# The swap of rotary halves: a permutation matmul replaced by VectorE products and ScalarE copies between groups of 32 partitions

## The chip, the cores and the metric

The kernel runs on all eight cores of one Trainium2 chip. Each core computes 2048 of the 16,384 tokens (batch 2, sequence 8192) and the 128 tokens before them again, so no core waits for another. The time of a run is that of the slowest core in microseconds (us). TensorE (PE) does the matrix products, VectorE (DVE), ScalarE (ACT) and GpSimd (POOL) the elementwise work, and SyncE's queue (SP) starts most transfers.

## The reference, cut to what matters

```python
x = x + 0.5 * swiglu(rmsnorm(x, g1), w_gate1, w_up1, w_down1)
h = rmsnorm(x, g_mix)
glu_a, glu_b, q, k, v, g_conv, g_attn = split(h @ w_in)
conv_out = (silu(layernorm(depthwise_conv31(glu_a * sigmoid(glu_b))))) @ w_proj
q, k = rope(q), rope(k)                # 16 query heads, 4 key/value heads of 64
attn_out = window_attention(q, k, v, sinks) @ w_o        # window of 128
x = x + (sigmoid(g_conv) * conv_out + sigmoid(g_attn) * attn_out) @ w_out
x = x + 0.5 * swiglu(rmsnorm(x, g2), w_gate2, w_up2, w_down2)
out = rmsnorm(x, g_final)

def rope(x):                           # half = 32
    x1, x2 = x[..., :32], x[..., 32:]
    return concat([x1 * cos - x2 * sin, x2 * cos + x1 * sin])
```

## The kernel before, in words

Everything is kept transposed: channels on the 128 partitions, tokens along the free axis. A core works through four tiles (t = 0 to 3) of 512 tokens. A tile passes three parts: FFN 1 (`f_a`, matmuls with inputs xnF and Hh), the mixers (`m_norm`, `m_rest`, inputs xnM, RR, cT, qa, cvo), and FFN 2 (`f_b`, xnF and Hh again). The mixers of tile t run beside FFN 2 of tile t-1 and FFN 1 of tile t+1, so TensorE has FFN matmuls to put between those of the mixers. Weights are streamed through six buffers `wa` and five `wd`: first as float32 over POOL's queue (wall, wd), later from bfloat16 copies over SP's queue (wac, wdc).

The mixers of a tile run in this order: GLU and convolution (lines 852 to 861), keys and values (`kv`, line 688), the sums of the layer norm (`ln_sums`), eight chunks of queries (line 866), sixteen attention units (`attn`, line 779) with one `ln_apply` in every second, gates and projections, and the output projection.

Rotary embedding is done on chunks of 128 channels, two heads, so a half is a group of 32 partitions. Per tile there are ten chunks (two of keys, eight of queries), and tile 0 has two more with 128 tokens. `rope_start` (line 671) projects a chunk into a PSUM bank `pa`, and ScalarE copies it as bfloat16 into a buffer `sq`. `rope_finish` (line 678) multiplies it with the permutation matrix `pswap` on TensorE into a second bank `pr`; VectorE forms t1 = pa * scale * cos and t2 = pr * sin, and GpSimd adds them into `qa` or `kT`. The sign of the sine is in its table (line 1031). For queries, the projection of the next chunk is emitted ahead of the finish of the last one (lines 870 to 873).

The mixers share five PSUM banks, handed out in turn (`bM5`, line 442). In the query loop the order of requests is pa0, pa1, pr0, pa2, pr1, pa3, pr2, and so on. FFN work beside the mixers has three banks (`bF`). The mixers' float32 buffers `tm` are four, also in turn.

The order of work is set before the kernel runs, by a planner (`Plan.schedule`, line 184). Each operation is a task with a planned duration (VectorE 0.7 where none is given, ScalarE 0.62, GpSimd 1.28, a 512-column matmul 0.217), and `join` ties several into one task. The planner keeps a clock for each engine and always places the task that can start first; of equal ones, the one with the lower key (its place in the tile). It adds 0.25 between engines. The result is one fixed list per engine, and on the chip each engine takes its list strictly in order, waiting at semaphores. Those come from `_deps` (line 62), which follows the emitted order and adds one rule that the planner's `_link` (line 154) does not have: an engine that reads a PSUM bank waits for reads of that bank by other engines that were emitted earlier (lines 68 to 71).

Of the kernel before, what the change touches and what calls it, by code (L numbers as in the profile page):

```python
# [7 lines left out]
F32, BF16, I32 = mybir.dt.float32, mybir.dt.bfloat16, mybir.dt.int32  # L8
AF = mybir.ActivationFunctionType
ALU = mybir.AluOpType  # L10
# [326 lines left out]
def build_nc():  # L337
    nc = bass.Bass("TRN2", target_bir_lowering=False)
    dt = nc.dram_tensor
# [6 lines left out]
    w2_d = dt("w2", [8, 128, 1024], F32, kind="ExternalInput").ap()  # L346
    misc_d = dt("misc", [128, 32], F32, kind="ExternalInput").ap()
    ident_d = dt("ident", [128, 128], F32, kind="ExternalInput").ap()
    pswap_d = dt("pswap", [128, 128], F32, kind="ExternalInput").ap()
    outT_d = dt("outT", [D, TOK], F32, kind="ExternalOutput").ap()  # L350
    wac_d = dt("wac", [NBLK_A + 8, 128, 2048], BF16, kind="Internal").ap()
    wdc_d = dt("wdc", [32, 128, 11 * 128], BF16, kind="Internal").ap()
# [2 lines left out]
    with ExitStack() as es:  # L355
        def sb(name, shape, dtype):
            return es.enter_context(nc.sbuf_tensor(name, shape, dtype))
# [8 lines left out]
        POOL = Eng(nc.gpsimd, mksem("s_pool"), 1.28)  # L366
        SP = Eng(nc.sync, mksem("s_sp"))
        G = Plan()
        op, dma = G.op, G.dma
        tt, stt, ts = nc.vector.tensor_tensor, nc.vector.scalar_tensor_tensor, nc.vector.tensor_scalar  # L370
        act, ptt, mm = nc.scalar.activation, nc.gpsimd.tensor_tensor, nc.tensor.matmul
# [27 lines left out]
        wd_hs = [mksem(f"s_wdh{i}") for i in range(ND)]  # L399
        tmF = Banks([(sb(f"tf{i}", [128, NT], F32), Buf()) for i in range(4)])  # L400
        tmM = Banks([(sb(f"tm{i}", [128, NT], F32), Buf()) for i in range(4)])
        sqt = Banks([(sb(f"sq{i}", [128, NT], BF16), Buf()) for i in range(2)])
        sqF = Banks([(sb(f"sx{i}", [128, NT], BF16), Buf()) for i in range(2)])
        accF, accL, accQ = [(sb(f"acc{i}", [128, NT], F32), Buf()) for i in range(3)]
        S = sb("S", [128, 8, 132], F32); S_b = bufs(2)
# [5 lines left out]
        sin_t = sb("sin_t", [128, NT], F32); sin_b = Buf()  # L411
        masks = sb("masks_sb", [128, 4, 128], BF16); masks_b = Buf()
        ident = sb("ident_sb", [128, 128], BF16); ident_b = Buf()
        pswap = sb("pswap_sb", [128, 128], BF16); pswap_b = Buf()
        ones = sb("ones_sb", [128, 128], BF16); ones_b = Buf()
        onesf = sb("onesf_sb", [128, 128], F32); onesf_b = Buf()
        cols = sb("cols_sb", [128, 9, 8], F32); cols_b = Buf()
        hcols = sb("hcols_sb", [128, 9, 8], F32); hcols_b = Buf()
        misc = sb("misc_sb", [128, 32], F32); misc_b = Buf()
# [22 lines left out]
        bM5 = Banks(every[3:8])  # L442
# [4 lines left out]
        def cdma(q, name, dst, src, buf, after=()):  # L447
            dma(q, mksem("s_c_" + name), [(dst, src)], rd=after, wr=(buf,))
# [27 lines left out]
        def ACTF(out, in_, func, rd, wr, t=None, **kw):  # L476
            op(ACT, partial(act, out=out, in_=in_, func=func, **kw), rd, wr, t)

        def STT(out, in0, scalar, in1, op0, op1, rd, wr, t=None):
            op(DVE, partial(stt, out=out, in0=in0, scalar=scalar, in1=in1, op0=op0, op1=op1), rd, wr, t)  # L480
# [7 lines left out]
        def TT(out, in0, in1, o, rd, wr, t=None):  # L488
            op(DVE, partial(tt, out=out, in0=in0, in1=in1, op=o), rd, wr, t)
# [7 lines left out]
        def MM(out, lhsT, rhs, start, stop, rd, wr, t=None):  # L497
            op(PE, partial(mm, out, lhsT=lhsT, rhs=rhs, start=start, stop=stop), rd, wr, t)
# [172 lines left out]
        def rope_start(use, sub, xn_t, xn_bufs, N, scale=1.0):  # L671
            pa, pab = bM5.get()
            proj(pa, pab, use, sub, xn_t, xn_bufs, N)
            qb, qbb = sqt.get()
            ACTF(qb[:, 0:N], pa[:, 0:N], AF.Copy, (pab,), (qbb,), scale=scale)
            return pa, pab, qb, qbb, scale

        def rope_finish(item, c_t, c_b, s_t, s_b, out, obufs, N):
            pa, pab, qb, qbb, scale = item
            pr, prb = bM5.get()  # L680
            MM(pr[:, 0:N], pswap[:], qb[:, 0:N], True, True, (pswap_b, qbb), (prb,))
            t1, t1b = tmM.get()
            t2, t2b = tmM.get()
            STT(t1[:, 0:N], pa[:, 0:N], scale, c_t[:, 0:N], ALU.mult, ALU.mult, (pab, c_b), (t1b,))
            TT(t2[:, 0:N], pr[:, 0:N], s_t[:, 0:N], ALU.mult, (prb, s_b), (t2b,))
            PTT(out, t1[:, 0:N], t2[:, 0:N], ALU.add, (t1b, t2b), obufs)

        def kv(t):
# [242 lines left out]
        load_pos(HALO, NT, cos_t, cos_b, (H_b[4],))  # L931
        load_x(1, (H_b[8],))
        cdma(POOL, "ident", ident[:], ident_d, ident_b, (H_b[11],))
        cdma(POOL, "pswap", pswap[:], pswap_d, pswap_b)
        cdma(POOL, "masks", masks[:], masks_d, masks_b)
        G.key = -0.6
        rope_tables(HALO, cos_h, cosh_b, sin_h, sinh_b)
# [19 lines left out]
def _pack_shared(inp):  # L957
    f = np.float32
    w_in = np.asarray(inp["w_in"][0], f)
    bnds = np.cumsum([1024, 1024, 1024, 256, 256, 1024, 1024])  # L960
    glu_a, glu_b = w_in[:, :bnds[0]], w_in[:, bnds[0]:bnds[1]]
    wq, wk, wv = w_in[:, bnds[1]:bnds[2]], w_in[:, bnds[2]:bnds[3]], w_in[:, bnds[3]:bnds[4]]
    g_conv, g_attn = w_in[:, bnds[4]:bnds[5]], w_in[:, bnds[5]:bnds[6]]

    def rot(wh):
        n = wh.shape[1] // 64
        return wh.reshape(D, n, 2, 32)[:, :, ::-1, :].reshape(D, n * 64)

    def qchunk(w, qc):
        gp, i = qc // 4, qc % 4  # L970
        h0, h1 = 4 * (2 * gp) + i, 4 * (2 * gp + 1) + i
        return np.concatenate([w[:, h0 * 64:(h0 + 1) * 64], w[:, h1 * 64:(h1 + 1) * 64]], axis=1)

    blocks = []

    def ffn_blocks(wg, wu):
        for b in range(NFC):
            blocks.append(np.concatenate([wg[:, 128 * b:128 * b + 128], wu[:, 128 * b:128 * b + 128]], axis=1))

    ffn_blocks(np.asarray(inp["ffn1_w_gate"][0], f), np.asarray(inp["ffn1_w_up"][0], f))  # L980
    blocks.append(wk)
    blocks.append(wv)
    for j in range(4):
        blocks.append(np.concatenate([qchunk(wq, 2 * j), qchunk(wq, 2 * j + 1)], axis=1))
    for cc in range(8):
        blocks.append(np.concatenate([glu_a[:, 128 * cc:128 * cc + 128], glu_b[:, 128 * cc:128 * cc + 128]], axis=1))
    w_cp = np.asarray(inp["conv_w_proj"][0], f)
    w_o = np.asarray(inp["attn_w_o"][0], f)
    perm = np.zeros(D, np.int64)
    for hc in range(8):  # L990
        gp, i = hc // 4, hc % 4
        for e in range(2):
            h = 4 * (2 * gp + e) + i
            perm[hc * 128 + e * 64:hc * 128 + e * 64 + 64] = np.arange(h * 64, h * 64 + 64)
    w_o_p = w_o[perm, :]
    for dc in range(8):
        blocks.append(np.concatenate([g_conv[:, 128 * dc:128 * dc + 128], g_attn[:, 128 * dc:128 * dc + 128]], axis=1))
        blocks.append(np.concatenate([w_cp[:, 128 * dc:128 * dc + 128], w_o_p[:, 128 * dc:128 * dc + 128]], axis=1))
    w_out = np.asarray(inp["w_out"][0], f)
    for j in range(4):  # L1000
        blocks.append(w_out[:, 256 * j:256 * j + 256])
    ffn_blocks(np.asarray(inp["ffn2_w_gate"][0], f), np.asarray(inp["ffn2_w_up"][0], f))
    assert len(blocks) == NBLK_A
    wall = np.stack([np.asarray(b, f).reshape(8, 128, 256).transpose(1, 0, 2).reshape(128, 2048) for b in blocks], axis=0)
    wall = np.ascontiguousarray(wall)
    wd = np.stack([np.asarray(inp["ffn1_w_down"][0], f), np.asarray(inp["ffn2_w_down"][0], f)], axis=0)
    wd = wd.reshape(2, 2, 11, 128, 8, 128).transpose(0, 4, 1, 3, 2, 5)
    wd = np.ascontiguousarray(wd.reshape(32, 128, 11 * 128))

    gate_b = np.asarray(inp["gate_b"][0], f)  # L1010
    vecs = [inp["ffn1_norm"][0], inp["mix_norm"][0], inp["ffn2_norm"][0], inp["final_norm"], inp["conv_dw_b"][0],
            inp["conv_ln_g"][0], inp["conv_ln_b"][0], gate_b[:1024], gate_b[1024:]]
    cols = np.stack([np.asarray(v, f).reshape(8, 128) for v in vecs], axis=0)
    cols = np.ascontiguousarray(cols.transpose(2, 0, 1))
    dw = np.zeros((32, D), f)
    dw[32 - CW:] = np.asarray(inp["conv_dw_w"][0], f)
    dw = dw.reshape(8, 4, 8, 4, 32)
    w2 = np.zeros((8, 4, 32, 4, 8, 32), f)
    ii = np.arange(32)
    w2[:, :, ii, :, :, ii] = dw.transpose(4, 2, 1, 3, 0)  # L1020
    w2 = np.ascontiguousarray(w2.reshape(8, 128, 1024))
    misc = np.zeros((128, 32), f)
    p = np.arange(128)
    inv_freq = (np.float32(10000.0) ** (-np.arange(32, dtype=f) / np.float32(32))).astype(f)
    misc[:, 0] = inv_freq[p % 32]
    misc[:, 1] = np.where((p % 64) < 32, -1.0, 1.0)
    sinks = np.asarray(inp["attn_sinks"][0], f)
    misc[:, 2] = EPS
    misc[:, 3] = LN_EPS
    misc[:, 4] = np.pi / 2  # L1030
    for gp in range(2):
        for i in range(4):
            for e in range(2):
                misc[:, 16 + gp * 8 + (i // 2) * 4 + e * 2 + i % 2] = sinks[4 * (2 * gp + e) + i]
    ident = np.eye(128, dtype=f)
    pswap = np.zeros((128, 128), f)
    mm = np.arange(128)
    pswap[np.where((mm % 64) < 32, mm + 32, mm - 32), mm] = 1.0
    return dict(wall=wall, wd=wd, cols=cols, w2=w2, misc=misc, ident=ident, pswap=pswap)

def _masks(first):
    q = np.arange(128)[:, None]
# [35 lines left out]
```

How the kernel before makes its waits and increments, by code:

```python
    def wait(self, sem, val):  # L40
        if val <= 0:
            return
        if sem is self.sem:
            if val > sem.n or not SAME_ENGINE_SYNC or self.no_self:
                return
        if self.known.get(sem, 0) >= val:
            return
        self.e.wait_ge(sem.h, val)
        self.known[sem] = val
# [29 lines left out]
def emit_op(eng, fn, rd=(), wr=()):  # L79
    for s, v in _deps(rd, wr, eng.sem).items():
        eng.wait(s, v)
    inst = fn()
    eng.sem.n += 1
    inst.then_inc(eng.sem.h, 1)
    ev = eng.sem.n
    for b in wr:
        b.w = {eng.sem: ev}
        b.r = {}
    for b in rd:
        if b.r.get(eng.sem, 0) < ev:
            b.r[eng.sem] = ev
# [1 line left out]
def emit_dma(q, dsem, moves, rd=(), wr=()):  # L93
    for s, v in _deps(rd, wr, None).items():
        q.wait(s, v)
    q.wait(dsem, dsem.n)
    for out_ap, in_ap in moves:
        q.e.dma_start(out=out_ap, in_=in_ap).then_inc(dsem.h, 16)
        dsem.n += 16
    for b in wr:
        b.w = {dsem: dsem.n}
        b.r = {}
    for b in rd:
        b.r[dsem] = dsem.n
```

## Time and profile before

| | us |
|---|---|
| median of 3 runs | 1834.73 (1834.13 to 1840.92) |
| the profiled execution | 1835.85 |
| its span, slowest core (core 7) | 1834.8 |
| spans of the eight cores | 1814.7 to 1834.8 |
| PE busy | 1668.5 (91%) |
| DVE, ACT, POOL busy | 709.8, 651.3, 690.0 (39%, 35%, 38%) |

The span is the time from a core's first to its last instruction; about 1 us of the execution lies outside it. PE's busy time is modelled for overlapping matmuls: a lone 512-column matmul is shown with 379 ns, but in a dense row they start some 216 ns apart. The same holds in a smaller way for DVE and ACT, whose next instruction can start before the last has ended. So durations and distances between starts are both read. All rows below are of core 7.

### The profile page before, as it was taken

The numbers are of one execution on the slowest core, as the hardware profiler recorded it, in microseconds if no ns is written. First come the engines' busy times: TensorE is split into PE (matmuls) and PEld (weight loads), VectorE is DVE, ScalarE is ACT, GpSimd is POOL, SyncE is SP. The second block draws the span as 40 slices with busy tenths as digits, with TensorE's granted clock in tenths as the row PEclk, the third lists the DMA queues.
The fourth block names the chain that finished last, engine by engine and source line by source line (L and its number), as shares of the span: only waits on it lengthen the run. The fifth ranks groups of instructions, "written<-read, shape, count | busy, mean of one in ns | idle before, by whom it ended". The sixth has DMA issues, their size and how long they took to land.

```text
span 1834.8 us, 29585 instructions; the slowest of 8 cores (1814.7 to 1834.8 us)
## 1 busy us (share of the span) xinstructions
PE 1668.5 (91%) x9060; PEld 747.1 (41%) x9060; DVE 709.8 (39%) x1180; ACT 651.3 (35%) x1396; POOL 690.0 (38%) x727
## 2 busy tenths in 40 slices
PE   6989878898987889789999999999998999998997
PEld 3545334343433334334443344444443444443442
DVE  3431523753152266332225267532214356524212
ACT  3211413653221266333322247543222257513221
POOL 1113136754331396423331377422322277322221
PEclk9989888899998999899999999999999999998987
DMA  9987899669898897976754987673443953444432
GB/s 180 195 183 139 177 202 196 166 163 222 165 201 194 197 188 153 178 200 199 198 146 145 230 225 176 156 236 133 158 140 113 247 164 121 148 141 142 155 102 100
DMA packets 121001, 315.39 MB, mean 172 GB/s; under 512 B 14864, under 2 KB 36624, under 8 KB 120848
## 3 DMA queue, kind: packets, MB, share of 16 engines
q1 hardware_dynamic: 94784, 231.47, 40.0%
q0 software_dynamic: 25344, 80.95, 27.6%
q8 instruction: 78, 1.28, 0.3%
q10 hardware_dynamic: 720, 1.09, 0.2%
q14 instruction: 75, 0.61, 0.1%
HBM read 327.01 MB, written 67.37 MB: 215 GB/s over the span
## 4 chain that ended last, share of the span: by engine, by line
PE 76%; DMA 14%; issue 3%; DVE 2%; ACT 2%; POOL 2%; SPq 1%; DVEq 0%; ACTq 0%; POOLq 0%
PE ps L501 70%; PE ps L82 4%; DMA wa<-wall 4%; DMA X<-xT 2%; DMA wa<-wac 1%; DMA outT<-tf 1%; DMA wd<-wd 1%; SPq L98 1%; DMA wdc<-wd 1%; DMA RR<-ush 1%; DMA ush<-uT 1%; DMA ush<-S 1%; PE ps L699 1%; DMA wac<-wa 1%; DMA wd<-wdc 1%
## 5 line engine op out<-in xcount | busy, mean ns | idle before, releaser
L501 PE MATMUL ps<-xnF,wa 128*128 128x512 bf16 x2816 | 669.0, 393 | 40.4 <-DMA wa<-wall 17.2
L501 PEld LDWEIGHTS ps<-xnF,wa 128*128 128x128 bf16 x2816 | 274.2, 100 | 395.6 <-issue 119.1
L501 PE MATMUL ps<-Hh,wd 128*128 128x512 bf16 x1408 | 341.3, 391 | 17.0 <-DMA wd<-wd 10.0
L501 PE MATMUL ps<-xnM,wa 128*128 128x512 bf16 x1344 | 313.8, 385 | 6.2 <-DMA wa<-wac 3.8
L82 ACT ACTIVATE tf<-ps 128x512 f32<-128x512 f32 x304 | 180.0, 595 | 346.4 <-PE ps L501 320.0
L82 POOL TENSOR_TENSOR Hh<-tf 128x512 bf16<-128x512 f32 x128 | 165.1, 1292 | 200.6 <-PE ps L501 126.7
L82 DVE SCALAR_TENSOR_TENSOR tf<-tf,ps 128x512 f32<-128x512 f32 x176 | 120.2, 684 | 307.8 <-PE ps L501 269.2
L501 PEld LDWEIGHTS ps<-Hh,wd 128*128 128x128 bf16 x1408 | 136.9, 100 | 187.3 <-issue 59.1
L501 PEld LDWEIGHTS ps<-xnM,wa 128*128 128x128 bf16 x1344 | 130.9, 99 | 177.1 <-issue 31.4
L82 DVE SCALAR_TENSOR_TENSOR X<-ps,X 128x512 f32<-128x512 f32 x96 | 66.3, 691 | 224.4 <-PE ps L501 215.6
L98 POOL DMA_DIRECT2D wa<-wall x117 | 65.2, 559 | 217.5 <-PE ps L501 177.1
L82 ACT ACTIVATE S<-S,sm 128x129 f32<-128x129 f32 x256 | 103.1, 403 | 65.4 <-DVE sm L82 46.8
L82 POOL TENSOR_TENSOR acc<-acc,tf 128x512 f32<-128x512 f32 x56 | 70.9, 1265 | 109.7 <-ACT tf L82 106.6
L82 DVE SCALAR_TENSOR_TENSOR tm<-tm,ps 128x512 f32<-128x512 f32 (+1 forms) x86 | 50.1, 584 | 156.9 <-PE ps L501 150.6
L82 POOL TENSOR_TENSOR P<-S,sm 128x512 bf16<-128x512 f32 x64 | 67.0, 1046 | 80.0 <-DVE sm L82 41.7
L82 POOL TENSOR_TENSOR acc<-acc,tm 128x512 f32<-128x512 f32 x56 | 70.7, 1263 | 67.7 <-ACT tm L82 67.5
L82 POOL TENSOR_TENSOR cvo<-tm 128x512 bf16<-128x512 f32 x32 | 40.5, 1267 | 136.9 <-DVE tm L82 136.7
L82 POOL TENSOR_TENSOR cvo<-cvo,acc 128x512 f32<-128x512 f32 x64 | 83.2, 1305 | 10.2 <-ACT acc L82 9.0
L501 PE MATMUL ps<-RR,wa 128*32 128x512 bf16 x1024 | 65.5, 403 | 23.1 <-DMA RR<-ush 19.0
L82 ACT ACTIVATE tm<-ps,hcols_sb 128x512 f32<-128x512 f32 x64 | 43.4, 686 | 111.5 <-PE ps L501 102.1
L82 ACT ACTIVATE tf<-X 128x512 f32<-128x512 f32 x56 | 35.1, 626 | 132.7 <-DVE X L82 106.6
L82 ACT ACTIVATE tm<-cvo 128x512 f32<-128x512 f32 (+1 forms) x67 | 39.5, 593 | 117.6 <-DVE cvo L82 114.2
(100 smaller groups left out, 1548.7 us busy)
## 6 DMA issues: line engine op xcount, KB each, us to landing
wa<-wac SPq DMA_DIRECT2D x195, 512.0 KB, 4.7
wa<-wall POOLq DMA_DIRECT2D x117, 512.0 KB, 9.0
wac<-wa SPq DMA_DIRECT2D x78, 512.0 KB, 8.0
wd<-wdc SPq DMA_DIRECT2D x80, 352.0 KB, 4.1
RR<-ush SPq DMA_DIRECT2D x128, 135.0 KB, 5.2
wd<-wd POOLq DMA_DIRECT2D x48, 352.0 KB, 7.5
wdc<-wd SPq DMA_DIRECT2D x32, 352.0 KB, 5.5
X<-xT SPq DMA_DIRECT2D x28, 256.0 KB, 9.7
```

Of the source, the lines that this page charges most:

```text
L82: inst = fn()
L98: q.e.dma_start(out=out_ap, in_=in_ap).then_inc(dsem.h, 16)
L501: op(PE, lambda: mm(out, lhsT=pick(use.slot), rhs=rhs, start=start, stop=stop), rd, wr, t, use)
L699: op(PE, lambda kc=kc: mm(pst[:, 0:256], lhsT=xn_t[:, kc, c0:c0 + 128], rhs=uv.slot[:, kc, 0:256], start=(kc == 0), stop=(kc == 7)), (xn_b ...
```

## The change: what it does

The matrix `pswap`, its transfer and its bfloat16 copy go, and with them the copies into `sq` and the 42 permutation matmuls. In their place, in `rope_finish`:

- for the lower 64 partitions, two VectorE instructions on 32 partitions each read `pa` at the partition group that is the other half of the pair, multiply by scale and sine, and write t2;
- for the upper 64 partitions, two ScalarE copies on 32 partitions each bring the other half (float32, scaled) from `pa` into the bank `pr`, and one VectorE product over 64 partitions forms the rest of t2;
- t1 is as before, and is joined with the first two products into one task of the planner. The two copies are another joined task, planned at 0.6 each.

The copies are now in `rope_finish`, so they are emitted after the next chunk's projection; `rope_start` holds the projection alone. The banks are asked for in the same order as before.

```diff
-        pswap = sb("pswap_sb", [128, 128], BF16); pswap_b = Buf()
-        sqt = Banks([(sb(f"sq{i}", [128, NT], BF16), Buf()) for i in range(2)])
...
         def rope_start(use, sub, xn_t, xn_bufs, N, scale=1.0):
             pa, pab = bM5.get()
             proj(pa, pab, use, sub, xn_t, xn_bufs, N)
-            qb, qbb = sqt.get()
-            ACTF(qb[:, 0:N], pa[:, 0:N], AF.Copy, (pab,), (qbb,), scale=scale)
-            return pa, pab, qb, qbb, scale
+            return pa, pab, scale
 
         def rope_finish(item, c_t, c_b, s_t, s_b, out, obufs, N):
-            pa, pab, qb, qbb, scale = item
-            pr, prb = bM5.get()
-            MM(pr[:, 0:N], pswap[:], qb[:, 0:N], True, True, (pswap_b, qbb), (prb,))
+            pa, pab, scale = item
             t1, t1b = tmM.get()
             t2, t2b = tmM.get()
+            pr, prb = bM5.get()
+            G.join(True)
+            for d in (64, 96):
+                ACTF(pr[d:d + 32, 0:N], pa[d ^ 32:(d ^ 32) + 32, 0:N], AF.Copy, (pab,), (prb,), t=0.2 + 0.4 * N / 512, scale=scale)
+            G.join(False)
+            G.join(True)
+            for d in (0, 32):
+                STT(t2[d:d + 32, 0:N], pa[d ^ 32:(d ^ 32) + 32, 0:N], scale, s_t[d:d + 32, 0:N], ALU.mult, ALU.mult, (pab, s_b), (t2b,))
             STT(t1[:, 0:N], pa[:, 0:N], scale, c_t[:, 0:N], ALU.mult, ALU.mult, (pab, c_b), (t1b,))
-            TT(t2[:, 0:N], pr[:, 0:N], s_t[:, 0:N], ALU.mult, (prb, s_b), (t2b,))
+            G.join(False)
+            TT(t2[64:128, 0:N], pr[64:128, 0:N], s_t[64:128, 0:N], ALU.mult, (prb, s_b), (t2b,))
             PTT(out, t1[:, 0:N], t2[:, 0:N], ALU.add, (t1b, t2b), obufs)
...
-        cdma(POOL, "pswap", pswap[:], pswap_d, pswap_b)
```

## Rows read from the trace of the kernel before

**Rows 1.** The page: TensorE's and DMA's lines of the 40 slices.
```profile
PE   6989878898987889789999999999998999998997
PEclk9989888899998999899999999999999999998987
DMA  9987899669898897976754987673443953444432
```

**Rows 2.** The page: the chain that ended last, by engine.
```profile
PE 76%; DMA 14%; issue 3%; DVE 2%; ACT 2%; POOL 2%; SPq 1%; DVEq 0%; ACTq 0%; POOLq 0%
```

**Rows 3.** Groups by form: operation, out<-in, count | busy us, mean ns | idle before, releasers.
```profile
L82 PE MATMUL ps<-sq,pswap_sb 128*128 128x512 bf16 x40 | 15.2, 379 | 0.6 <-ACT sq L82 0.6
L82 PE MATMUL ps<-sq,pswap_sb 128*128 128x128 bf16 x2 | 0.4, 216 | 0.1
L82 ACT ACTIVATE sq<-ps 128x512 bf16<-128x512 f32 x40 | 23.7, 594 | 31.8 <-PE ps L501 31.1 <-DVE tm L82 0.8
L82 ACT ACTIVATE sq<-ps 128x128 bf16<-128x128 f32 x2 | 0.6, 278 | 1.3 <-PE ps L699 1.3
L82 DVE SCALAR_TENSOR_TENSOR tm<-ps,cos_t 128x512 f32<-128x512 f32 x40 | 27.6, 690 | 30.1 <-PE ps L501 16.8 <-POOL qa L82 9.9 <-PE ps L699 3.1
L82 DVE SCALAR_TENSOR_TENSOR tm<-ps,S 128x128 f32<-128x128 f32 x2 | 0.6, 291 | 1.7 <-PE ps L82 1.0 <-PE ps L699 0.7
L82 ACT ACTIVATE tm<-ps,hcols_sb 128x512 f32<-128x512 f32 x64 | 43.4, 686 | 111.5 <-PE ps L501 102.1 <-POOL cvo L82 4.8 <-DVE tm L82 3.6
```

**Rows 4.** Timeline of TensorE, queries of tile 3: start, us, operation.
```profile
1494.17 0.38 PE L82 MATMUL ps<-sq,pswap_sb 128*128 128x512 bf16 x1
1494.38 1.89 PE L501 MATMUL ps<-xnM,wa 128*128 128x512 bf16 x8
1496.11 0.38 PE L82 MATMUL ps<-sq,pswap_sb 128*128 128x512 bf16 x1
...
1549.48 5.35 PE L501 MATMUL ps<-xnF,wa 128*128 128x512 bf16 x24
```

**Rows 5.** Timeline of VectorE, tile 2, queries and start of attention.
```profile
1086.35 0.69 DVE L82 SCALAR_TENSOR_TENSOR tm<-ps,cos_t 128x512 f32<-128x512 f32 x1 [0.99 <-POOL qa L82]
1086.96 0.68 DVE L82 TENSOR_TENSOR tm<-ps,sin_t 128x512 f32<-128x512 f32 x1
1087.58 0.69 DVE L82 SCALAR_TENSOR_TENSOR tm<-ps,cos_t 128x512 f32<-128x512 f32 x1
1088.55 0.69 DVE L82 TENSOR_TENSOR tm<-ps,sin_t 128x512 f32<-128x512 f32 x1 [0.28 <-PE ps L82]
...
1090.77 6.46 DVE L82 SCALAR_TENSOR_TENSOR cT<-tm,cvo 128x512 bf16<-128x512 f32 x1 [0.93 <-ACT tm L82]
1097.15 0.72 DVE L82 COPY_PREDICATED S<-masks_sb,ps 128x512 f32<-128x512 uint16 x1
1097.97 0.69 DVE L82 TENSOR_REDUCE sm<-S 128x4 f32<-128x516 f32 x1
...
1101.11 0.18 DVE L82 RECIPROCAL sm<-sm 128x4 f32<-128x4 f32 x1 [0.66 <-ACT S L82]
```

**Rows 6.** Timeline of ScalarE, the same stretch.
```profile
1098.75 0.41 ACT L82 ACTIVATE S<-S,sm 128x129 f32<-128x129 f32 x1 [5.28 <-DVE sm L82]
...
1100.82 0.19 ACT L82 ACTIVATION_READ_ACCUMULATOR S<-S,sm 128x1 f32 x1
...
1101.39 1.07 ACT L82 ACTIVATE tf<-ps 128x512 f32<-128x512 f32 x2
```

**Rows 7.** Windows: PE, PEld, DVE, ACT, POOL busy, clock, DMA, GB/s; queries of tiles 1, 2, 3.
```profile
647.00:662.40 15.40, 14.72 (x69) 6.47 (x67) 9.23 (x15) 7.11 (x12) 15.17 (x15) 1.00 0.97 193
1075.00:1085.00 10.00, 10.00 (x48) 4.50 (x47) 7.44 (x12) 4.17 (x7) 9.79 (x10) 1.00 0.80 168
1490.00:1504.20 14.20, 14.20 (x69) 6.27 (x66) 9.30 (x14) 6.21 (x12) 12.91 (x12) 1.00 0.39 128
```

**Rows 8.** Timeline of TensorE, start of attention, tiles 0, 1, 2, then tile 3.
```profile
327.97 0.61 PE L82 MATMUL ps<-kT,qa 64*128 64x256 bf16 x4 [3.30 <-DVE S L82]
328.52 8.09 PE L501 MATMUL ps<-xnF,wa 128*128 128x512 bf16 x24
...
354.45 0.75 PE L82 MATMUL ps<-PT,V 128*64 128x256 bf16 x4 [3.34 <-DVE PT L82]
...
673.30 0.38 PE L82 MATMUL ps<-ident_sb,P 128*128 128x128 bf16 x4 [2.66 <-POOL P L82]
...
1098.01 0.41 PE L82 MATMUL ps<-kT,qa 64*128 64x256 bf16 x4 [4.02 <-DVE S L82]
1098.36 7.04 PE L501 MATMUL ps<-xnF,wa 128*128 128x512 bf16 x24
...
1534.53 1.89 PE L501 MATMUL ps<-xnF,wa 128*128 128x512 bf16 x8 [0.51 <-ACT tf L82]
```

More of the change, by code:

```diff
@@ L348, in build_nc @@
     ident_d = dt("ident", [128, 128], F32, kind="ExternalInput").ap()
-    pswap_d = dt("pswap", [128, 128], F32, kind="ExternalInput").ap()
     outT_d = dt("outT", [D, TOK], F32, kind="ExternalOutput").ap()
@@ L1035, in _pack_shared @@
     ident = np.eye(128, dtype=f)
[L1036 to L1039, printed above, removed]
+    return dict(wall=wall, wd=wd, cols=cols, w2=w2, misc=misc, ident=ident)
 def _masks(first):
```

## The prediction

> **What bounds the kernel now.** I read the page's slices first. TensorE is busy nine tenths or more in nearly all of the second half, while DMA falls to three to five tenths there; in the first half DMA is at seven to nine tenths and TensorE has gaps [rows 1]. The chain of waits puts 76% on PE and 14% on DMA [rows 2]. So the second half, tiles 2 and 3, is bound by TensorE, and the first partly by weight transfers. A matmul taken away is worth its full place on PE only where PE is dense.
>
> Then the groups by form, for what the change touches [rows 3], the timelines of the query stage for the distances between starts [rows 4 to 6], and the windows for the room beside it [rows 7]. In the query stages PE is full (14.72 of 15.40, 10.00 of 10.00, 14.20 of 14.20), DVE is at 60, 74 and 65% and POOL at 99, 98 and 91%. Last, what PE waits for where attention begins [rows 8].
>
> **What it removes.** 42 matmuls, 40 of them of 512 columns. The profile gives one 379 ns, but that is a modelled end: from one permutation matmul to the next, nine matmuls apart, are 1496.11 - 1494.17 = 1.94 us, so one costs 0.216 [rows 4]. 40 x 0.216 = 8.6 us, and two of 128 columns, at a quarter to the full distance, 0.1 to 0.4. Together 8.8 us off PE. Their weight loads lie under other matmuls. PE waited only 0.6 us for their inputs in all [rows 3], so no stall goes with them. Where PE is at half clock the saving doubles, but the query stages of tiles 1 to 3 are at 1.00 [rows 7]. The transfer of the matrix is one of hundreds and I give it nothing; at most it frees one short slot on POOL's queue.
>
> **What it adds.** None of the new operations is in the trace: all work on 32 or 64 partitions, and three move data between partition groups. For a VectorE product of 512 columns the nearest rows are t1 and t2, at 0.69 us each and 0.61 from start to start [rows 3, 5]. If time followed the amount of data, the 128x128 form at 0.29 would be the nearest below; if a shifted read were as bad as the worst product here, it would be the 6.46 of cT [rows 5]. I take 0.61 between starts and 0.69 for the last, since that row has the same columns, types and memories. For a ScalarE copy of 512 columns the rows are 0.594 alone, two in 1.07 (0.48 between starts), 0.686 with a bias and 0.278 for 128 columns [rows 3, 6]; I take two in 1.07.
>
> Per chunk of 512 columns VectorE goes from two instructions (1.22) to four (2.44), which is 40 x 1.22 = 49 us more on an engine with 1,125 us idle. ScalarE goes from one copy to two, 40 x 0.48 = 19 us more. GpSimd has the same adds. None of this is on PE by itself. But in the query stage a chunk cost PE 1.94, and costs it 1.73 now (nine places less one), against 2.44 on VectorE: there VectorE becomes the slower one, and eight chunks take it 19.5 us instead of the some 14 seen for the whole stage. The planner knows this, for it counts 4 x 0.7 = 2.8 a chunk, and will put FFN matmuls into the difference, 8 x (2.8 - 1.73) = 8.6 us, two or three FFN blocks of 3.46. Those are not lost: in tile 3 a lot of FFN work is left when the attention begins, and the attention units are spread over it by their keys. If that cover were gone it would be 8.6 us a tile, 34 in all.
>
> The Trainium skill, VectorE: DVE Perf Modes, section "Two Vector instructions with no wait between them", speaks against the change: an instruction whose input or output starts in another group of 32 partitions than the one before it starts only when all earlier ones have ended. Every one of the four instructions of a chunk does so, and the next instruction after them. The trace before has no such case: its starts are 0.61 apart at a duration of 0.69 [rows 5]. By the rule the four take 4 x 0.69 = 2.8 and the loop below 0.16 more a chunk, 5 us over the kernel before cover.
>
> **What it moves.** The planner does not know that readers of one PSUM bank on two engines take turns; the semaphores enforce it. Both engines now read `pa`, the copies on ScalarE first as they can start first, and VectorE's three after them. Also the bank for `pr` of chunk n is the one that held `pa` of chunk n-1 (five banks in turn), so ScalarE can't begin before VectorE has finished its three instructions of chunk n-1. That makes a loop through two engines. From the end of VectorE's three for one chunk: 0.1 to ScalarE (1098.66 to 1098.75), 1.07 for the two copies, 0.1 back (1101.01 to 1101.11), then 0.61 + 0.61 + 0.69 = 1.91, in all 3.2 us [rows 5, 6]. The one product of 64 partitions fits under the copies. The plan has 2.8 for it. So a chunk ends 0.4 later than planned each time, and the first one 1.2 later: 1.2 + 7 x 0.4 = 4.0 us a tile, 16 us for four tiles. Before, ScalarE's one copy was out of the way long before VectorE came (VectorE idled 0.3 to 1.0 us a chunk [rows 5]), so this did not show.
>
> Queued behind the waiting VectorE and ScalarE instructions are the FFN's tanh, copy and product, which free the three FFN banks, and the next attention unit. PE takes its list in order, so it stands when one of those banks or the first queries are late. Between nothing (the FFN's VectorE instructions that lie inside the loop fill the wait, and PE has 1.07 a chunk of other work) and the full 4.0 us a tile, I take half, 2.0 a tile, as the loop has about one FFN instruction of VectorE every second chunk. That is 8 us. The keys' two chunks a tile have value projections behind them on PE and I give them nothing; without that cover it is 1.2 each.
>
> **The sum.** -8.8 + 8 = -0.8 us on the profiled 1835.85, which itself is 1.1 above the median; on the median 1834.73 this is 1834.
>
> **Rivals.**
>
> *The saving stands.* For it: VectorE has room in all windows, and FFN instructions fill the loop. Then PE has 8.8 us less to do: 1826. More is possible. The stalls where attention begins come from a single product, cT from two SBUF operands, that takes 6.46 instead of 0.68 while GpSimd runs without a pause [rows 5]; they stop PE for 3.30, 3.34, 2.66 and 4.02 us, and after two of them 24 matmuls take 8.09 or 7.04 instead of 5.35 [rows 4, 8]. In the change, GpSimd's adds come 2.8 apart instead of 1.94 and its queue is emptier by then. If two of those stalls go, with 1.7 to 2.7 of slow clock each, it is 10 us more: 1816. Against it: such stalls depend on how the lists happen to meet, and can as well grow.
>
> *The loop reaches PE whole; the kernel is slower.* Place: VectorE and ScalarE taking turns on `pa` in the eight query chunks of each tile. Price: 4 x 4.0 = 16 us, with the late first queries making one stall of 3 us or more at the start of attention, after which matmuls ran slowly for 1.7 to 2.7 us [rows 4, 8], 4 x 2.2 = 9. 16 + 9 - 8.8 = +16: 1851. With VectorE's starts 0.69 apart it is 4 x 1.1 = 5 more, 1856. It decides from 2.2 us of stall a tile on, where it has eaten the saving; from 4.5 a tile it is measurable. For it: the order is fixed, and PE is dense, so what is late by more than the plan's margin shows at once. Against it: the plan's 0.25 between engines is 0.1 on the chip, and its 0.7 is 0.61.
>
> *It is hidden anyway.* In tiles 0 and 1 the PE waits for weights after the mixers, so time saved or lost there returns in a transfer wait. Only tiles 2 and 3 count, 20 matmuls, -4.3 us, or with half the loop -0.3: 1830 to 1834, inside my own case.
>
> **Chances and range.** Within 0.5% (9.2 us, about what a measurement of this kernel can tell from no change) lie my forecast and the hidden case, 1825.6 to 1843.9: 0.38. The saving with fewer stalls, faster by over 0.5%, 0.29: the plain saving falls just inside the bound, and needs some luck with the stalls. Slower by over 0.5%, 0.33. The range goes from 1816 (saving and two stalls gone) to 1858 (the loop whole, held starts); the likeliest case's own is 1826 to 1844.
>
> **What would show it.** The forecast is right if PE has 42 matmuls less, DVE's busy time grows by about 40 x 1.38 = 55 us and ACT's by some 20 to 24, VectorE's copies of the pattern three-then-one show 3.2 a chunk or more with waits on ScalarE between, and PE has new stalls of 1 to 3 us a tile in and just after the query stage. If the three products follow each other without a wait for ScalarE, the loop is wrong and the first rival holds. If PE stands 4 us or more a tile on queries or FFN banks, and the granted clock falls behind it, the second holds. It would all be wrong if a product on 32 partitions with a shifted read took far from 0.69, or if the new lists shift weight transfers so that DMA waits of PE change by more than 10 us.

## The result, and the profile after

The changed kernel is slower: the ratio to the kernel before is 1.0204 (95% interval 1.0167 to 1.0241), some 38 us. Three executions took 1869.8 to 1875.5 us, the profiled one 1873.54 (span 1872.5, core 5). In the other three one die ran at a granted clock of 0.79 to 0.84, which the kernel before showed too in some of its runs, and every time and ratio in this document leaves such runs out.

The changed kernel's page, to be laid beside [rows 1, 2]: the 40 slices and the chain that ended last.

```profile
PE   6989767897987879889999887998999998999897
PEclk9999889999998989999999999999998999999898
DMA  9988988769898868875654966675443853353533
...
PE 69%; DMA 15%; DVE 6%; issue 4%; ACT 3%; SPq 2%; POOL 1%; DVEq 0%; ACTq 0%; POOLq 0%
```

PE has lost a tenth or two where the queries and the start of attention of a tile lie (slices 7, 15, 23 to 25 and 34; five other slices lost a tenth and three gained one), and the chain has 6% on DVE in place of 2%, 7% less on PE. The groups by form that the change made (operation, out<-in, shapes, count | busy us, mean ns | idle before and what ended it):

```profile
L82 DVE SCALAR_TENSOR_TENSOR tm<-ps,sin_t 32x512 f32<-32x512 f32 x80 | 54.5, 681 | 38.2 <-ACT ps L82 21.0 <-PE ps L498 8.2 <-POOL acc L82 2.7
L82 DVE TENSOR_TENSOR tm<-ps,sin_t 64x512 f32<-64x512 f32 x40 | 27.8, 694 | 5.7 <-ACT ps L82 4.6
L82 DVE SCALAR_TENSOR_TENSOR tm<-ps,cos_t 128x512 f32<-128x512 f32 x40 | 27.7, 691 | 1.3
L82 ACT ACTIVATE ps<-ps 32x512 f32<-32x512 f32 x80 | 45.4, 568 | 47.2 <-DVE tm L82 30.6 <-PE ps L498 9.8 <-PE ps L701 2.8
```

A product on 32 partitions takes 681 ns, as long as one on 128 (690 in [rows 3]); what a VectorE or ScalarE instruction costs here goes by its 512 columns, not by its partitions. New is the idle time: 21.0 us of VectorE's ended by ScalarE, 30.6 us of ScalarE's ended by VectorE. That is the loop. In tile 3 it looks like this on VectorE (start, us, operation, idle before):

```profile
1541.57 1.47 DVE L82 SCALAR_TENSOR_TENSOR tm<-ps,sin_t 32x512 f32<-32x512 f32 x2 [0.77 <-ACT ps L82]
1543.07 0.69 DVE L82 SCALAR_TENSOR_TENSOR tm<-ps,cos_t 128x512 f32<-128x512 f32 x1
1543.79 0.69 DVE L82 TENSOR_TENSOR tm<-ps,sin_t 64x512 f32<-64x512 f32 x1
1545.25 1.47 DVE L82 SCALAR_TENSOR_TENSOR tm<-ps,sin_t 32x512 f32<-32x512 f32 x2 [0.77 <-ACT ps L82]
```

and on ScalarE:

```profile
1540.17 1.23 ACT L82 ACTIVATE ps<-ps 32x512 f32<-32x512 f32 x2 [2.52 <-DVE tm L82]
...
1543.86 1.23 ACT L82 ACTIVATE ps<-ps 32x512 f32<-32x512 f32 x2 [1.73 <-DVE tm L82]
```

A chunk takes 1545.25 - 1541.57 = 3.68 us, where the forecast had 3.2. Two terms were short: the copies take 1.23 a pair and not 1.07, and the three products 2.19 (1541.57 to 1543.76) and not 1.91, as their starts are 0.71 to 0.79 apart. On TensorE, the same stretch:

```profile
1531.74 7.07 PE L498 MATMUL ps<-xnM,wa 128*128 128x512 bf16 x32
1541.16 3.12 PE L498 MATMUL ps<-xnM,wa 128*128 128x512 bf16 x8 [2.35 <-DVE tm L82]
1544.08 2.38 PE L498 MATMUL ps<-xnF,wa 128*128 128x512 bf16 x8
1546.30 1.89 PE L498 MATMUL ps<-xnM,wa 128*128 128x512 bf16 x8
1548.03 5.34 PE L498 MATMUL ps<-xnF,wa 128*128 128x512 bf16 x24
1557.90 0.54 PE L82 MATMUL ps<-kT,qa 64*128 64x256 bf16 x4 [4.53 <-DVE tm L82]
1559.35 3.25 PE L498 MATMUL ps<-xnF,wa 128*128 128x512 bf16 x8 [0.91 <-DVE tf L82]
```

PE projects four chunks at once, then stands until a bank is free; it has 32 FFN matmuls to do after that, and stands 4.53 us in front of the first scores. The 8 matmuls at 1541.16 and at 1559.35 take 3.12 and 3.25 instead of 1.89: after each of the two stalls the granted clock was at the lower of its two levels, 1.2 GHz, for a while (its mean is 0.59 from 1541.1 to 1544.1 and 0.57 from 1559.3 to 1562.6). The four stages from the last value projection to the first scores, in windows (PE, PEld, DVE, ACT, POOL busy, clock, DMA share, GB/s), with the sum of the same stages before in the last line:

```profile
298.60:338.10 39.50, 31.78 (x150) 14.58 (x150) 27.71 (x46) 22.48 (x39) 27.38 (x28) 1.00 0.75 148
647.70:681.10 33.40, 29.87 (x124) 12.73 (x124) 22.50 (x34) 19.70 (x31) 24.52 (x23) 0.90 0.67 142
1096.00:1131.50 35.50, 26.50 (x122) 11.68 (x122) 25.24 (x38) 20.70 (x32) 25.84 (x23) 0.96 0.56 131
1523.10:1557.90 34.80, 27.91 (x122) 12.33 (x123) 23.96 (x36) 19.70 (x31) 23.49 (x19) 0.95 0.34 106
sum 143.20, PE 116.05 PEld 51.32 DVE 99.42 ACT 82.59 POOL 101.24; mean PE 29.01 PEld 12.83 DVE 24.85 ACT 20.65 POOL 25.31
...
sum 102.50, PE 101.85 PEld 48.24 DVE 53.58 ACT 53.57 POOL 77.18; mean PE 25.46 PEld 12.06 DVE 13.39 ACT 13.39 POOL 19.29
```

Before, the same four stages took 102.5 us with PE busy for 101.85. Now they take 143.2 with 27 us of it idle. Over the whole kernel, the gaps in PE's timeline by what ended them, mean of the eight cores: VectorE 23.2 us before and 53.9 after (+30.7), ScalarE 33.4 and 34.6, GpSimd 19.4 and 21.2, transfers 78.7 and 81.8; in all 155.9 and 192.7. So PE has 37 us more idle time and 8.8 us less work, and the mean span grew by 34.8. Of the 7 us between, 3 are clock: PE's busy time at a lowered clock, times what the clock lacked to 1, is 58.5 us before and 61.8 after. The rest was not traced.

### The profile page after: what moved, and what is told of

Read it like the earlier page. It is cut to its first block, busy times and chain, and to the rows that moved or that the text cites. A ratio compares the mean times of both kernels' runs of the same rounds, so it can differ in the third digit from the quotient of the medians.

```text
span 1872.5 us, 29671 instructions; the slowest of 8 cores (1840.5 to 1872.5 us)
## 1 busy us (share of the span) xinstructions
PE 1655.4 (88%) x9018; PEld 740.6 (40%) x9018; DVE 764.9 (41%) x1264; ACT 674.4 (36%) x1438; POOL 690.2 (37%) x726
## 3 DMA queue, kind: packets, MB, share of 16 engines
q8 instruction: 77, 1.26, 0.3%
## 4 chain that ended last, share of the span: by engine, by line
PE 69%; DMA 15%; DVE 6%; issue 4%; ACT 3%; SPq 2%; POOL 1%; DVEq 0%; ACTq 0%; POOLq 0%
PE ps L498 65%; PE ps L82 4%; DVE tm L82 4%; DMA wa<-wall 3%; DMA wa<-wac 2%; DMA X<-xT 2%; DMA ush<-uT 2%; ACT ps L82 2%; SPq L98 2%; DMA RR<-ush 1%; DMA wdc<-wd 1%; DMA wd<-wd 1%; DMA ush<-S 1%; DVE S L82 1%; DMA wd<-wdc 1%
## 5 line engine op out<-in xcount | busy, mean ns | idle before, releaser
L498 PE MATMUL ps<-Hh,wd 128*128 128x512 bf16 x1408 | 331.1, 383 | 17.9 <-DMA wd<-wdc 9.7
L98 POOL DMA_DIRECT2D wa<-wall x117 | 65.5, 561 | 227.4 <-PE ps L498 192.7
```

What stands on the lines that cost most here:

```text
L98: q.e.dma_start(out=out_ap, in_=in_ap).then_inc(dsem.h, 16)
L498: op(PE, lambda: mm(out, lhsT=pick(use.slot), rhs=rhs, start=start, stop=stop), rd, wr, t, use)
```

## The experiments

Two questions: does the loop cost the time, and through what. All ratios are to the kernel before on the same chip; 1% is 18.4 us.

**The two sides of the change, one at a time.** `b_noswap` is the kernel before without copies and matmuls:

```diff
-            ACTF(qb[:, 0:N], pa[:, 0:N], AF.Copy, (pab,), (qbb,), scale=scale)
-            MM(pr[:, 0:N], pswap[:], qb[:, 0:N], True, True, (pswap_b, qbb), (prb,))
-            TT(t2[:, 0:N], pr[:, 0:N], s_t[:, 0:N], ALU.mult, (prb, s_b), (t2b,))
+            TT(t2[:, 0:N], pa[:, 0:N], s_t[:, 0:N], ALU.mult, (pab, s_b), (t2b,))
```

> The kernel before with the 42 permutation matmuls and the 42 ScalarE copies in front of them left out; VectorE multiplies pa itself by the sine, so the halves are not exchanged. Everything else, and the order in which banks are asked for, is as before. Theory 1 (the added loop between ScalarE and VectorE costs the time, the removed matmuls bring what was forecast): 8.8 us less than before, within 3 us, as PE is dense in the query stages. Rival 2 (the lists of the planner re-roll by far more than 8.8 us whenever a task changes, and the 38 us are such a re-roll): anything from 20 faster to 20 slower than before.

Measured: 0.9871 (0.9845 to 0.9897), 24 us faster, nearly three times what was expected. `b_nomm` keeps the copies and leaves out the matmuls alone:

> The kernel before without the 42 permutation matmuls but with the ScalarE copies (whose result nobody reads); VectorE multiplies pa itself by the sine, so the halves are not exchanged. Leaving out both gave 24 us. Theory A (TensorE's place is the saving, PE being the bound): 18 to 26 us faster than before, the copies being free. Theory B (the copies and their turns on pa cost the other 15): 7 to 12 us faster.

Measured: 0.9957 (0.9933 to 0.9981), 8 us. The forecast's first term, 8.8 us for the 42 matmuls, stands. The copies on ScalarE are worth another 16 us in the kernel before (9 to 22 by the two intervals). PE's idle time ended by VectorE is 23.9 us with them and 15.8 without, which is half of it; where the other half goes was not found.

`b_dve2` adds VectorE's share of the change to the kernel before and leaves the swap on TensorE:

```diff
+            G.join(True)
+            for d in (0, 32):
+                STT(t2[d:d + 32, 0:N], pa[d ^ 32:(d ^ 32) + 32, 0:N], scale, s_t[d:d + 32, 0:N], ALU.mult, ALU.mult, (pab, s_b), (t2b,))
             STT(t1[:, 0:N], pa[:, 0:N], scale, c_t[:, 0:N], ALU.mult, ALU.mult, (pab, c_b), (t1b,))
+            G.join(False)
```

> The kernel before, whole, with the two shifted VectorE products on 32 partitions added ahead of t1 and joined with it (the later full product overwrites their result). VectorE has then more work a chunk (four instructions, 64 us more in all) than in the changed kernel, but ScalarE has one copy a chunk, emitted early, and the second bank is filled by TensorE. Theory 1 (it is the loop: copies on ScalarE wait for VectorE of the chunk before, VectorE waits for the copies): at most a third of the loss, so 0 to 13 us slower than before. Rival 3 (it is VectorE's load in the query stage, with or without ScalarE): 30 us or more slower. The starts of the shifted products are 0.72 to 0.75 us apart if the hold between partition groups is what stretched them.

Measured: 1.0066 (1.0043 to 1.0089), 12 us slower. The shifted products start 0.79 apart and t1 0.71 after the second, so the mean is as expected. VectorE's busy time, 758.9 us, is nearly that of the changed kernel (764.9), so a third of the loss comes with the load and two thirds come with something else.

**Undoing the loop by banks.** `a_banks` asks for `pr` next to `pa`:

```diff
             pa, pab = bM5.get()
+            bank = bM5.get()
             proj(pa, pab, use, sub, xn_t, xn_bufs, N)
```

> The changed kernel with the bank pr asked for right after pa, before the projection. With five banks in turn, pr of chunk n is then the bank that held pa of chunk n-2 and not n-1, so ScalarE's copies need not wait for VectorE's three instructions of the chunk before. All instructions are the same. Theory 1: a chunk takes VectorE's own 2.9 us in place of 3.68, its waits for ScalarE of 0.77 a chunk are gone, and half to all of the 38 us come back: 1840 to 1855. Rival 3 (VectorE's load): no gain over 5 us, 1868 to 1876.

Measured: 1.0183 (1.0149 to 1.0217). A miss: in the second half of the stage a chunk did take 2.95 us (1544.88 to 1547.83 in tile 3, without a wait), but nothing came back. PE's idle time ended by VectorE is 47.5 us in place of 53.9, but that ended by ScalarE is 41.8 in place of 34.6 and by transfers 87.3 in place of 81.8. So the loop's length is not the price by itself.

**Telling the planner.** `a_link` gives the planner the rule of the semaphores:

```diff
         for b in rd:
             k.after.update(b.pw)
+            if b.psum:
+                k.after.update(a for a in b.pr if a.eng is not k.eng)
```

> The changed kernel, with the planner told of the rule that the semaphores follow: a task that reads a PSUM bank comes after the reads of other engines that were made before it. No instruction and no semaphore rule changes, only the order of the lists. Theory 1 (PE stands because the planner put too little FFN work beside a loop that it did not see): the loop stays at 3.7 us a chunk, PE's stalls at the queries and the start of attention shrink, and half to all of the loss comes back: 1838 to 1855. Rival 3 (the loop's length itself is the cost, whatever lies beside it): 1865 to 1880.

Measured: 1.0037 (1.0014 to 1.006). Four fifths of the loss is gone, with every instruction still there. PE's timeline in the query stage of tile 3:

```profile
1509.77 7.07 PE L500 MATMUL ps<-xnM,wa 128*128 128x512 bf16 x31
1516.68 1.89 PE L500 MATMUL ps<-xnF,wa 128*128 128x512 bf16 x8
1518.41 1.89 PE L500 MATMUL ps<-xnM,wa 128*128 128x512 bf16 x8
1520.13 3.62 PE L500 MATMUL ps<-xnF,wa 128*128 128x512 bf16 x16
1523.59 1.89 PE L500 MATMUL ps<-xnM,wa 128*128 128x512 bf16 x8
1525.53 10.31 PE L500 MATMUL ps<-xnF,wa 128*128 128x512 bf16 x47
1535.77 0.39 PE L82 MATMUL ps<-kT,qa 64*128 64x256 bf16 x4
```

and its four stages together:

```profile
sum 141.40, PE 136.97 PEld 63.13 DVE 104.92 ACT 95.95 POOL 120.57; mean PE 34.24 PEld 15.78 DVE 26.23 ACT 23.99 POOL 30.14
```

The stages are as long as in the changed kernel (141.4 and 143.2), but PE is busy for 137 us of them in place of 116, so 4 us of them are idle in place of 27. Between the last value projection and the first scores the lists have 104, 72, 88 and 88 FFN matmuls of 512 columns in tiles 0 to 3, against 64, 48, 48 and 48 in the changed kernel and 32, 24, 32 and 24 before. (`b_dve2` has 64, 48, 48 and 48 as well, but its stages are 18 us shorter in all, and only 5 us of them are idle.) 144 more, at 0.216 us, are 31 us, which is also the gain (31 us). That the two agree so well is chance: in the two versions with a later key below the same sum gives 17 us for a gain of 27, and 36 for 30.

Two controls ask whether any new plan moves the time so far. `b_link` has the same two lines in the kernel before; `b_roll` has GpSimd planned at 1.26 in place of 1.28.

> Control: the kernel before, with only the planner told that readers of one PSUM bank on two engines take turns. Theory 1 (blindness of the planner matters where the copy and the product meet late, as in the changed kernel): before had slack there, so within 8 us of before. Rival 4 (the rule helps any version equally, and the gain of some 27 us with it in the changed kernel is no sign of the loop): 15 us or more faster than before.

> Control for the re-roll: the kernel before with the planner's duration of GpSimd operations at 1.26 in place of 1.28, nothing else; the measured mean is 1.27. All lists are planned anew. Rival 2 (any new plan moves the time by tens of us): 15 us or more either way. Theory 1: within 6 us of before.

Measured: 0.9988 (0.9967 to 1.0008) and 0.9986 (0.9952 to 1.0019), neither clear of 1. For the kernel before, a new plan by itself moved the time by less than 9 us either way. For the changed kernel no such control was run, and the next group shows that small changes of its planned durations move more.

**Right durations.** `a_linkcost` and `a_cost` plan the copies at 0.62 and the three products at 0.75 each, with and without the rule; `b_dve2cost` does that for `b_dve2`.

```diff
-...AF.Copy, (pab,), (prb,), t=0.2 + 0.4 * N / 512, scale=scale)
+...AF.Copy, (pab,), (prb,), t=0.62 * N / 512, scale=scale)
-...ALU.mult, ALU.mult, (pab, s_b), (t2b,))
+...ALU.mult, ALU.mult, (pab, s_b), (t2b,), t=0.75)
```

> The changed kernel with the planner told of the readers' turns and of the durations that the trace shows: 0.62 a copy on 32 partitions, 0.75 for each of the three products (start to start 0.72 to 0.75 when the partition group changes). Theory 1: the plan then meets the chip, PE's idle time that VectorE ends goes from 31 us (with the rule alone) towards the 22 us of before, and the time to 1830 to 1845, not slower than with the rule alone. Rival 3 (what is left is the length of the loop, not the plan): no gain over the rule alone, 1840 to 1850.

> The changed kernel with the measured durations in the plan (0.62 a copy, 0.75 a shifted product and t1) and without the rule on readers. The plan has then 2.95 a chunk on VectorE, the chip 3.68. Theory 1 with the turns as the larger part: the loss of 38 us shrinks by a third at most, 1857 to 1872. Rival 5 (it was the durations, and the rule only lengthened the plan in the same way): as fast as with both, 1837 to 1848.

> The kernel before with the two shifted products added, planned now at 0.75 for each of the three joined instructions. Without this it was 12 us slower than before. Theory 1: the 12 us are the 0.15 a chunk by which the plan fell short, and it comes to within 5 us of before. Rival 3: still 9 to 15 us slower, as the load stays.

Measured: 1.0023 (0.9998 to 1.0048) with the rule, 1.0306 (1.0274 to 1.0338, from two runs) without, and for `b_dve2cost` two runs of 1864.55 and 1868.02 us, which give no interval, against 1853.0 to 1856.5 for `b_dve2` on another chip (the kernel before has a median of some 1838 us on the chip of `b_dve2cost` and some 1841 on that of `b_dve2`). With the rule, PE's idle time that VectorE ends did not fall as expected: it is 32 us, as with the rule alone (33). The other two are plain misses, and they refuted the theory in its first form, that PE stands because the plan is shorter than the chip: better durations made it worse. `a_dve` and `a_dvecost` say the same. All four shifted products are on VectorE, no engine takes turns on `pa`, and the second is planned at 3.75 a chunk, where the chip takes 3.81:

```diff
-            for d in (64, 96):
-                ACTF(pr[d:d + 32, 0:N], pa[d ^ 32:(d ^ 32) + 32, 0:N], AF.Copy, ...)
-            for d in (0, 32):
+            for d in (0, 32, 64, 96):
                 STT(t2[d:d + 32, 0:N], pa[d ^ 32:(d ^ 32) + 32, 0:N], ...)
-            TT(t2[64:128, 0:N], pr[64:128, 0:N], s_t[64:128, 0:N], ALU.mult, (prb, s_b), (t2b,))
```

> The changed kernel with all four shifted products on VectorE (five instructions a chunk, 3.7 us) and no ScalarE copies; the bank is still asked for and left unused. No engine takes turns with another on pa. Planned at 3.5, so the plan misses only 0.2 a chunk, 8 us in all, against 0.9 a chunk in the changed kernel. Theory 1 (turns that the plan does not know): faster than the changed kernel by 10 us or more, 1845 to 1862, though VectorE has 29 us more to do. Rival 3 (VectorE's load in the query stage): slower than the changed kernel, 1875 to 1890.

> The version with all shifted products on VectorE, planned at 0.75 for each of the five instructions (3.75 a chunk, the chip takes 3.7) in place of 0.7. No turns between engines, so this tells whether a plan short by 0.2 a chunk costs what was seen (34 us slower than before). Theory 1 (PE's stalls come from the plan falling behind the chip, whatever the reason): most of the loss goes, 1835 to 1850. Rival 3 (VectorE's load as such): 1865 to 1880.

Measured: 1.0185 (1.0154 to 1.0215) and 1.0209 (1.018 to 1.0238). With no loop at all the loss is the same. That doesn't make the loop free: a chunk still takes 3.81 us here, by VectorE's five instructions alone, where the loop had 3.68. What these versions share with the changed kernel stands in PE's timeline, here `a_dve` in tile 3:

```profile
1519.69 5.34 PE L498 MATMUL ps<-xnF,wa 128*128 128x512 bf16 x24
1524.87 12.25 PE L498 MATMUL ps<-xnM,wa 128*128 128x512 bf16 x56
1536.96 8.80 PE L498 MATMUL ps<-xnF,wa 128*128 128x512 bf16 x40
1553.68 0.61 PE L82 MATMUL ps<-kT,qa 64*128 64x256 bf16 x4 [7.92 <-DVE tm L82]
```

64 FFN matmuls, then nothing to do. In the lists it is 64, 32, 64, 64 with either duration, and for `b_dve2cost` 64, 48, 24, 32, less than the 64, 48, 48, 48 of `b_dve2`. That gave the second theory: the planner books VectorE for the rotary tasks, which have the lower key, without a hole; the FFN's product, which frees the three FFN banks, comes after them; so there are no FFN matmuls to lay beside. The rule would help because with it the plan shows VectorE waiting for ScalarE, and the FFN's products go into those holes. The traces agree with the theory here: VectorE does 5, 3, 4 and 4 of the FFN's products (tf<-tf,ps) in the four stages of `a_link`, but 2, 1, 2 and 1 in the changed kernel, no more than in the kernel before, whose stages are 9 to 12 us shorter.

The theory does not cover everything. `a_cost` has 64, 48, 56 and 56 FFN matmuls in its lists, more than the changed kernel, and 25 us of idle time in the stages, about the same, and yet it is 19 us slower. Its PE waits 9 us more on ScalarE and 5 more on VectorE, and the longer waits lie in the attention that follows. Why was not found.

**Only the order of the FFN's work.** `a_key`, `a_dvekey` and the control `b_key` change one number, the key of VectorE's rotary task:

```diff
+            keep, G.key = G.key, G.key + 0.3
             G.join(True)
             for d in (0, 32):
...
+            G.key = keep
             PTT(out, t1[:, 0:N], t2[:, 0:N], ALU.add, (t1b, t2b), obufs)
```

> The changed kernel, without the rule on readers and with the old durations; only VectorE's joined task of the rotary products has its key later by 0.3 of a tile, so that of tasks ready together VectorE takes the FFN's first. From the last value projection to the first score matmul the plan then has 72, 64, 80, 72 FFN matmuls of 512 columns in tiles 0 to 3, against 64, 48, 48, 48 in the changed kernel and 104, 72, 88, 88 with the rule. Theory 2 (the loss is that too few FFN matmuls stand beside the longer stage, because the FFN's VectorE work comes last there): about two thirds of the way to the version with the rule, 1845 to 1858. Theory 1 (the plan must know the turns): no gain over 8 us, 1864 to 1876.

> The version with all shifted products on VectorE, old durations, with the same later key on its joined task. FFN matmuls in the stage: 128, 80, 80, 104 against 64, 32, 64, 64. Theory 2: from 34 us slower than before to 10 to 22 slower, 1844 to 1858. Rival 3 (VectorE's load as such): still 28 or more slower, 1865 and up.

> Control: the kernel before with the later key on t1's task. The stage is full there, its FFN matmuls are 32, 24, 40, 24 against 32, 24, 32, 24. Theory 2: within 6 us of before. If it is 12 or more faster, the key is good by itself and says nothing on the change.

Measured: 1.0055 (1.0034 to 1.0075), 1.0024 (1.0006 to 1.0042), which is better than the 10 to 22 us of loss expected, and 1.0015 (0.9988 to 1.0041). The loop is untouched in `a_key`: VectorE's waits for ScalarE in it are 27.7 us against 27.3 in the changed kernel:

```profile
DVE tm L82 <- ACT ps L82: 27.7, 28, 2.4
```

and yet 27 of the 38 us are back. With all products on VectorE it is 30 of 34. No instruction differs between `a_key` and the changed kernel, or between `a_dvekey` and `a_dve`, so what the added operations cost hangs on the order of the lists, and putting the FFN's VectorE work ahead takes most of the cost away. The FFN's products in the four stages are 4, 3, 4 and 4 in `a_key`.

How the time comes back is only in part what the theory says. The four stages of `a_key` together:

```profile
sum 155.90, PE 134.82 PEld 58.69 DVE 112.94 ACT 88.76 POOL 112.60; mean PE 33.71 PEld 14.67 DVE 28.23 ACT 22.19 POOL 28.15
```

They hold more work, but they are also longer, and 21 us of them are still idle, 6 fewer than in the changed kernel. Over the whole kernel, mean of the eight cores, PE's idle time is 13 us less than in the changed kernel (179.3 for 192.7), and the mean granted clock is 0.961 in place of 0.952: what PE's busy time lost to a lowered clock is 49.1 us in place of 61.8, another 13. Together they make the 25 us by which the mean span is shorter. In `a_link` it is 17 us of idle time (175.5) and 8 of clock (53.6). So less idle time in the query stage is shown with the rule; with the key, half of the gain is clock, most of it in the attention after the stage. `a_key`'s PE still stands 42 us on VectorE over the kernel, against 33 with the rule. That this rest is the plan's ignorance of the turns is likely but not shown, as the two times differ by only 3 us.

**Better versions?** `a_early` has rule, durations, and the copies emitted with the projection:

> The changed kernel with rule and measured durations, and with the ScalarE copies emitted with the projection, as the copy of the kernel before is, and the bank pr asked for next to pa. The copies no longer wait for VectorE of the chunk before, and VectorE no longer for them; a chunk can take VectorE's own 2.95. FFN matmuls in the stage: 64, 88, 72, 72, enough for 8 chunks at 2.95. Theory 2: stage short and filled, 1832 to 1843, as fast as before or up to 6 us faster, since 8.8 us of TensorE work are gone. If the length of the stage doesn't matter once it is filled: the same as with rule and durations, 1838 to 1848.

Measured: 1.013 (1.0088 to 1.0171). A miss: PE stands 47 us on VectorE. Tile 3's stage is short and full as expected (29.5 us, no idle time), but tile 0's list has only 64 FFN matmuls in 40 us, and after the stage more stalls follow. Its lists have 296 FFN matmuls in the four stages, more than the 288 of `a_key`, which is faster, and it has the rule. So neither the count nor the rule is enough by itself. Why this plan comes out so was not pursued. The last two add the key to the versions with rule and durations, and to `a_dvecost`:

> The changed kernel with the rule on readers, the measured durations and the later key together; FFN matmuls in the stage 112, 96, 104, 96 against 104, 80, 80, 96 without the key. Theory 2: PE's idle time that VectorE ends goes from 31 us to 23 to 28, and the time to 0 to 0.2% of before, 1835 to 1844; if it were filled to the full, the 8.8 us of TensorE work would show as 1830.

> All shifted products on VectorE, with the key and 0.75 for each of the five instructions; FFN matmuls in the stage 144, 88, 88, 104 against 128, 80, 80, 104 without the durations. Theory 2: 0 to 0.3% above before, 1835 to 1846. If VectorE's load as such were the rest, 10 us or more above, as it has 67 us more work than before.

Measured: 1.0011 (0.9984 to 1.0037) and 1.0014 (0.9992 to 1.0037). Both are even with the kernel before and no better. In `a_linkkey` PE's idle time that VectorE ends stayed at 32 us, where 23 to 28 were expected.

Taken together, the changed kernel and its four versions with neither rule nor key (`a_banks`, `a_cost`, `a_dve`, `a_dvecost`) lie 1.8 to 3.1% above the kernel before, the six with rule, key or both 0.1 to 0.6%, and `a_early`, with the rule, 1.3%.

## Why the prediction was wrong

*The saving.* Right: 8.8 us forecast for the 42 matmuls, 8 measured with them alone left out. That the copies beside them cost nothing was wrong; with them gone too it was 24.

*The added operations.* Durations right to 5%: 681 and 694 ns for 690, 568 for 594. VectorE's busy time grew by 55.1 us (forecast 55), ScalarE's by 23.1 (forecast 20 to 24). Distances were short. The shifted products start 0.71 to 0.79 apart, where the forecast took 0.61. By the Trainium skill, VectorE: DVE Perf Modes, section "Two Vector instructions with no wait between them", an instruction that starts in another group of 32 partitions than the one before it is held until all earlier ones have finished; the forecast named this only as an alternative. The trace agrees with that rule: each start comes 0.03 to 0.10 us after the end of the instruction before, at least 0.71 apart, wherever the partition group changes, and 0.61 apart where it does not, here from t1 to another product on 128 partitions in tile 2:

```profile
1101.31 0.69 DVE L82 SCALAR_TENSOR_TENSOR tm<-ps,cos_t 128x512 f32<-128x512 f32 x1
1101.92 0.68 DVE L82 SCALAR_TENSOR_TENSOR acc<-ps,acc 128x512 f32<-128x512 f32 x1
```

In the loop the two copies on ScalarE don't overlap either: 1.23 for the pair, where two copies on 128 partitions took 1.07 [rows 6].

*The loop.* Right in place, order and cause: banks and readers in turn, 3.68 us a chunk for 3.2. That its lateness against the plan is what costs the time was wrong: without the loop (`a_dve`) the loss is the same, and with the loop whole (`a_key`) most of it is gone.

*The cover.* This is the step that failed. "The planner knows this, for it counts 4 x 0.7 = 2.8 a chunk, and will put FFN matmuls into the difference, 8 x (2.8 - 1.73) = 8.6 us, two or three FFN blocks of 3.46. Those are not lost". It put in 16 to 32 matmuls more a tile, 3.5 to 7 us, and there it stopped. The stage grew by 9 to 12 us a tile, so 27 us stayed empty in the four, where 1 us had been. The FFN's matmuls need their banks freed by VectorE, the slower engine of that stage now, and VectorE did no more FFN products in the longer stages than before (2, 1, 2 and 1). The price for a lost cover was in the text (8.6 a tile, 34 in all); I took it for hidden and booked 8 us of stall where VectorE ended 31 more. With that in place of the 8 the sum gives -8.8 + 31 = +22; PE's other waits grew by 6 and the clock took 3, which makes 31 of the 35 by which the mean span grew.

*The second rival* had the right sign and half of the size (1851 to 1856 for 1873), partly by luck: it had 16 us of stall for 31 and 9 us of slow clock for 3, and its cause, the loop reaching PE, is not the one that the runs show.

*The first rival* laid all four stalls at the start of attention to the product cT. One of them was read wrongly: the 2.66 in tile 1 was ended by GpSimd's P, and the two cT products there took 2.81 together.

*The hold on FFN banks.* Named ("PE stands when one of those banks or the first queries are late"), with half of it set aside because the loop has one FFN instruction every second chunk. The trace has 1 or 2 in the eight chunks of a tile. Half was a choice without a row behind it.

## What to carry to other kernels

When work is moved from the bounding engine to one with room on average, take the stage where it happens and ask which engine bounds it afterwards; if that engine also feeds the filler work, the filler can starve with it, whatever the average says. In a list scheduled ahead of time, count in the new order how many filler instructions stand beside the longer stage. The count pointed at the cause here, but it is no measure: `a_cost` and `a_early` have more filler than faster versions. More exact durations made this greedy planner's lists worse twice. An ordering rule that it lacked, or a priority for the work that frees TensorE's banks, brought back 27 to 31 us of 38.

## What the runs showed of the hardware

- VectorE instructions of 512 columns that change their partition group start 0.71 to 0.79 us apart, the same kind without a change 0.61, with durations of 0.68 to 0.69 in both.
- Two ScalarE copies on 32 partitions from PSUM to PSUM take 1.23 us in the loop; two on 128 partitions from PSUM to SBUF 1.07.
- Reading another partition group added nothing to the duration: 32 partitions of `pa` read for another group took 0.681, t1 on all 128 partitions 0.691.
